# A transformer trunk layer on one core: the weight ring goes from three whole blocks to three half blocks

## The chip, the cores and the metric

The kernel runs on one core of one Trainium2 chip. The metric is the device time of one launch in microseconds (us), lower is better. Before the change the median of three runs is 462.19 us (461.26 to 464.12).

## What is computed

One layer over 256 tokens of 1024 channels, in float32. The input is normalised and multiplied by one wide matrix `w_in`; three mixers work on slices of the product; their outputs are gated, projected and summed; a mixture of 32 experts follows, in four groups of eight, two experts for each token.

```python
xn = rms_norm(x, mix_norm)
(rnn_x, rnn_y, q, kc, vc, ksl, vsl, kwn, vwn, nsa_g, sc_b, sc_c, sc_h, merge_g) = split(xn @ w_in)
y_rnn = gelu(rnn_y) * rg_lru(conv4(rnn_x))
k_cmp, v_cmp = compress_blocks(kc, cmp_w1, ...), compress_blocks(vc, cmp_w1, ...)
y_nsa = g_cmp*Att_cmp + g_sel*Att_sel + g_win*Att_win
y_sc  = sc_b * conv3(sc_c * sc_h)
merged = sum_b sigmoid(gate_b) * (y_b @ P_b)        # P_b: w_rnn_out, w_nsa_out, w_sc_out
x = x + merged @ w_out
x = x + hierarchical_moe(rms_norm(x))               # 32 experts: w_gate, w_up [1024,256], w_down [256,1024]
```

The expert weights are 32 x 3 matrices of 1 MiB each, 96 MiB in all, and all of them are read.

## The kernel before

**Two stretches.** The first (the dense front, up to about 264 us) computes everything up to the router. The second (the experts) runs eight rounds of four experts, here called groups 0 to 7; each needs 8 MiB of gate and up weights and 4 MiB of down weights.

**Blocks and pieces.** The dense weights arrive in *blocks* of 2 MiB (512 columns of 1024 rows; `kvb` is narrower, 280 columns), in the order of the list `LOADS`: q, kva, kvb, rx, cmp, ry, sb, sc, sh, then ga0 gb0 w0, ga2 gb2 w2, ga1 gb1 w1, and wo0, wo1. Every block but cmp is worked on in two halves, the *pieces* (`PIECES`), numbered 0 to 37: q is 0 and 1, kva 2 and 3, kvb 4 and 5, rx 6 and 7, ry 8 and 9, and so on; w1 is 32 and 33, the four last are halves of wo0 and wo1. For float32 precision on TensorE a piece is split in two: ScalarE (ACT) copies it to `wh` (the high part, L750, signals `hi_ready`), VectorE (DVE) subtracts that from the piece to give `wl` (the low part, L1085, signals `lo_ready`). `wh` and `wl` hold two pieces each. TensorE (PE) then does 16 matmuls of 512 columns (or 32 of 256) with the high part and half as many with the low part of each piece (L1630, L1634, L1695). ACT and DVE do their copies at places written out by hand between their other work, so a copy that waits holds up what is written behind it.

**The ring.** `ring` has three slots of one block. All weight loads are issued by SyncE (SP), on its one DMA queue, in program order. Block i goes to slot i % 3 when both halves of block i-3 have been split (`used`: `lo_ready` at least the number of its second piece plus one). The block cmp (`cmp_w1`, rows of 128 floats, so 512 B at a time) is read by PE directly and is a block of the ring as well; it is free when `hidp` is full, the product at L1731. At the beginning SP issues x, q in three DMAs (L508), kva in two (L512), kvb, then waits for slots: rx after piece 1, cmp after piece 3, ry after piece 5, sb after piece 7.

**Expert buffers.** The loads of groups 0 and 1 have places that are partly other tensors' until late: `even[3]`, `even[4]`, `even[5]` are the ring slots 2, 0, 1; `even[0..2]` lie over attention and recurrence scratch; `odd[0..3]` over the split buffers and others. So some loads go early (`odd_half(3, 0)` and `down_half(1, 0, True)` before block sc, at 47 us), some in between, and those that lie in the ring only when the last blocks are through it: `first_group(3)` (2 MiB to `even[3]`), `down_half(0, 0)`, `(0, 2)`, `(0, 1)`, `(0, 3)` (1 MiB each). Gate and up weights of group 2 are issued when PE is through with the same buffer of group 0 (`kpair_done`), and so on for each later group.

**What PE does around it.** In order: q (pieces 0, 1), a small transpose, kva, kvb, transposes of `kdup`, rx, the product with cmp (L1731), transposes of the normalised q and k (L1741, L1747), ry, and so on. The normalised q and k come from DVE, which does them (L1191 to L1197, `qk_normed`) behind the low parts of pieces 6 and 7 and behind `cx` (L1183).

Of the kernel before, what the change touches and what calls it, by code (L numbers as in the profile page):

```python
# [24 lines left out]
P = 128  # L25
S, D = 256, 1024
TT = S // P
KD = D // P
W4 = 512
CT = W4 // P  # L30
# [28 lines left out]
LOADS = (["q", "kva", "kvb", "rx", "cmp", "ry", "sb", "sc", "sh"]  # L59
         + [f"{x}{b}" for b in BR for x in ("ga", "gb", "w")] + ["wo0", "wo1"])  # L60
LI = {n: i for i, n in enumerate(LOADS)}
# [20 lines left out]

SPLIT = [n for n in LOADS if n != "cmp"]

PIECES = [(n, hf) for n in SPLIT[:-2] for hf in range(2)] + [("wo0", 0), ("wo1", 0), ("wo0", 1), ("wo1", 1)]
# [5 lines left out]
MADE = {n: (f"{n}_0", f"{n}_1") if n[0] == "g" else (f"{n}0", f"{n}1") for n in SPLIT if n not in WB}  # L91
# [14 lines left out]
def trunk(nc, x, mix_norm, w_in, rnn_conv_w, rnn_conv_b, rg_wa, rg_ba, rg_wx, rg_bx, rg_lambda,  # L106
# [5 lines left out]
    with ctx:  # L112
# [7 lines left out]
        ring = sb("ring", [P, RING, SLOT])  # L120
# [48 lines left out]
        def part(area, at, shape):  # L169
# [48 lines left out]
                ring[:, 2, :], ring[:, 0, :], ring[:, 1, :]]  # L218
# [45 lines left out]
        slot_full = [sem(f"slot_full{i}") for i in range(RING)]  # L264
# [16 lines left out]
        kva_half, u_low, q_high = sem("kva_half"), sem("u_low"), sem("q_high")  # L281
# [32 lines left out]
        def copies(name):  # L314

            return 2 if name in ("cmp",) else 1

        def slot_count(name):

            i = LI[name]  # L320
            return 16 * sum(copies(LOADS[j]) for j in range(i % RING, i + 1, RING))

# [6 lines left out]

        def loaded(eng, name):  # L330
            eng.wait_ge(slot_full[LI[name] % RING], slot_count(name))

        def slot(name):
            return ring[:, LI[name] % RING, :]

# [7 lines left out]

        def used(eng, name):

            if (name, 1) in PI:
                eng.wait_ge(lo_ready, PI[name, 1] + 1)
            else:
                full(eng, "hidp")
# [16 lines left out]
        def halves(n, parts):  # L366


            name, hf = PIECES[n]
            if name in WB:  # L370
                src = slot(name).rearrange("p (k n) -> p k n", k=CT)[:, :, hf * CB:(hf + 1) * CB]
                return src, parts[:, n % 2, :].rearrange("p (k n) -> p k n", k=CT)
            w = {"kvb": KVB}.get(name, CB)
            src = slot(name)[:, hf * KH * w:(hf + 1) * KH * w].rearrange("p (k n) -> p k n", k=KH)
            return src, parts[:, n % 2, 0:KH * w].rearrange("p (k n) -> p k n", k=KH)
# [16 lines left out]
        def _(sp):  # L392
            def columns(name, c0, n):
                dst = slot(name)[:, 0:KD * n].rearrange("p (k n) -> p k n", k=KD)
                sp.dma_start(dst, win_v[:, :, c0:c0 + n]).then_inc(slot_full[LI[name] % RING], 16)

            def whole(name, w):
                dst = slot(name)[:, :].rearrange("p (k n) -> p k n", k=CT)
                sp.dma_start(dst, w[0].rearrange("(k p) n -> p k n", p=P)).then_inc(slot_full[LI[name] % RING], 16)

# [85 lines left out]
            for i, name in enumerate(LOADS):  # L486

                if name == "sc":
                    odd_half(3, 0)
                    down_half(1, 0, True)  # L490
                if name == "w2":
                    sp.wait_ge(yl_ready, 1)
                    down_half(1, 1, True)
                if name == "gb1":
                    sp.wait_ge(y_sc_ready, 1)
                    first_group(2)
                if name == "w1":
# [4 lines left out]
                if i >= RING:  # L502
                    used(sp, LOADS[i - RING])
                if name == "q":

                    dst = slot(name)[:, :].rearrange("p (k n) -> p k n", k=KD)
                    for k0, k1, done in ((0, 2, q_quarter[0]), (2, 4, q_quarter[1]), (4, 8, slot_full[0])):
# [1694 lines left out]
```

## Time and profile before

| what | value |
|---|---|
| median of three runs | 462.19 us (461.26 to 464.12) |
| span of the profiled execution, first to last instruction | 459.2 us |
| PE busy | 413.9 us, 90% of the span, 2701 matmuls |
| DVE, ACT, POOL busy | 217.9, 173.8, 40.0 us |
| HBM read | 144.83 MB, 318 GB/s over the span |
| SP's queue | 143.50 MB, 81.0% of 16 engines' span |
| mean granted TensorE clock | 0.959 of full speed |

A busy PE is a PE with matmuls in flight. A DMA share of 1.0 means that all 16 DMA engines moved data all the time. What matters is which of the two is full in which stretch, and what the queue holds at a given moment: transfers of one queue land in the order of their issue.

### The profile page before, as it was taken

How to read it: one execution, taken by the hardware profiler on the slowest of the kernel's cores; microseconds unless marked ns; L12 is line 12 of the kernel's file. 1: busy time of each engine (PE TensorE's matmuls, PEld its weight loads, DVE VectorE, ACT ScalarE, POOL GpSimd, SP SyncE). 2: the span in 40 equal slices, each digit the busy share in tenths (PEclk: the TensorE clock that was granted, in tenths of full speed). 3: DMA queues.
4: the chain of work that ended last, by engine and by line, in shares of the span. 5: the costliest groups of instructions: out<-in, count | busy, mean ns of one | idle time of the engine just before them, and what ended most of it. 6: DMA issues, size and time to landing. Idle time of an engine off the chain costs nothing.

```text
span 459.2 us, 6635 instructions
## 1 busy us (share of the span) xinstructions
PE 413.9 (90%) x2701; PEld 292.7 (64%) x2701; DVE 217.9 (47%) x336; ACT 173.8 (38%) x270; POOL 40.0 (9%) x66
## 2 busy tenths in 40 slices
PE   6999999999999999999999999999929659299586
PEld 3889999999878787888888853535512413225122
DVE  5658988487799994564584650211100201002011
ACT  6558429873764565344256331110201101002001
POOL 8420490000000000000003100000000000000000
PEclk9999999999999999999999899999968959889799
DMA  8997893254552578897589989999999999999996
GB/s 291 348 260 257 327 387 105 100 184 184 183 183 93 185 250 298 286 410 266 183 364 359 387 355 425 423 421 420 428 424 421 422 422 425 424 414 414 400 394 220
DMA packets 43613, 146.27 MB, mean 319 GB/s; under 512 B 2908, under 2 KB 6097, under 8 KB 34242
## 3 DMA queue, kind: packets, MB, share of 16 engines
q1 hardware_dynamic: 42272, 143.50, 81.0%
q10 hardware_dynamic: 562, 1.84, 1.1%
q0 software_dynamic: 752, 0.55, 0.5%
q8 instruction: 19, 0.31, 0.3%
q14 instruction: 8, 0.07, 0.0%
HBM read 144.83 MB, written 1.05 MB: 318 GB/s over the span
## 4 chain that ended last, share of the span: by engine, by line
PE 62%; SPq 15%; DMA 14%; DVE 5%; ACT 2%; issue 2%; DVEq 0%
PE psum L1634 17%; DMA ring<-in_exp_w_down 10%; PE psum L1630 10%; PE psum L1877 7%; SPq L413 6%; PE psum L1927 5%; SPq L461 3%; PE psum L2145 3%; PE psum L2048 3%; DMA a_att<-in_exp_w_down 3%; SPq L429 3%; PE psum L1695 2%; SPq L418 2%; PE psum L2017 2%; PE psum L1769 1%
## 5 line engine op out<-in xcount | busy, mean ns | idle before, releaser
L1085 DVE TENSOR_TENSOR wl<-ring,wh 128x2048 fp32r<-128x2048 f32 (+1 forms) x38 | 85.1, 2245 | 36.5 <-ACT wh L750 35.8
L750 ACT CAST wh<-ring 128x2048 fp32r<-128x2048 f32 (+1 forms) x37 | 69.1, 1868 | 52.6 <-PE psum L1634 21.0
L1574 DVE COPY mix<-psum 128x512 f32<-128x512 f32 (+1 forms) x8 | 5.3, 658 | 115.7 <-PE psum L2145 110.0
L1634 PE MATMUL psum<-wh,x_parts 128*128 128x512 f32 (+1 forms) x256 | 58.1, 379 | 0.2 <-ACT a_att L877 0.2
L1634 PEld LDWEIGHTS psum<-wh,x_parts 128*128 128x128 f32 x256 | 46.0, 188 | 9.1 <-issue 0.4
L1035 ACT COPY mix<-psum 128x512 f32<-128x512 f32 x8 | 4.7, 586 | 103.5 <-PE psum L2145 100.4
L2048 PE MATMUL psum<-a_att,mix 128*32 128x512 f32 x96 | 25.6, 693 | 18.0 <-DMA a_rnn<-in_exp_w_up 17.0
L1630 PE MATMUL psum<-x_parts,wh 128*128 128x256 f32 x320 | 40.5, 284 | 0.0
L1630 PEld LDWEIGHTS psum<-x_parts,wh 128*128 128x128 f32 x320 | 39.1, 192 | 0.1
L2048 PE MATMUL psum<-odd,mix 128*32 128x512 f32 x192 | 24.2, 661 | 10.0 <-DMA odd<-in_exp_w_up 8.8
L2145 PE MATMUL psum<-ring,a_moe 128*32 128x512 f32 x152 | 27.6, 658 | 5.1 <-DMA ring<-in_exp_w_down 5.1
L1634 PE MATMUL psum<-wl,x_parts 128*128 128x512 f32 (+1 forms) x128 | 30.1, 377 | 0.0
L2048 PEld LDWEIGHTS psum<-a_att,mix 128*32 128x32 f32 x96 | 7.0, 126 | 34.0 <-issue 34.0
L2017 PE MATMUL psum<-a_moe,tok 128*128 128x128 f32 x224 | 26.3, 275 | 0.3 <-DVE a_moe L1546 0.3
L2097 PE MATMUL psum<-mix,a_moe 128*128 128x512 f32 x56 | 26.3, 607 | 0.0
L1634 PEld LDWEIGHTS psum<-wl,x_parts 128*128 128x128 f32 x128 | 23.2, 188 | 4.4
L2017 PEld LDWEIGHTS psum<-a_moe,tok 128*128 128x128 f32 x224 | 25.6, 192 | 0.5 <-DVE a_moe L1546 0.5
L2048 PE MATMUL psum<-a_rnn,mix 128*32 128x512 f32 x48 | 25.5, 693 | 0.0
L2048 PE MATMUL psum<-ring,mix 128*32 128x512 f32 x48 | 25.5, 693 | 0.0
L2048 PEld LDWEIGHTS psum<-odd,mix 128*32 128x32 f32 x192 | 7.5, 120 | 24.5 <-issue 24.5
L729 POOL TENSOR_TENSOR tok<-a_rnn,a_att 128x512 f32<-128x512 f32 x4 | 5.2, 1300 | 183.3 <-DVE a_rnn L1448 179.9
L1630 PE MATMUL psum<-x_parts,wl 128*128 128x256 f32 x160 | 20.8, 283 | 0.0
(319 smaller groups left out, 629.7 us busy)
## 6 DMA issues: line engine op xcount, KB each, us to landing
ring<-in_w_in SPq DMA_DIRECT2D x11, 2048.0 KB, 7.8
ring<-in_exp_w_down SPq DMA_DIRECT2D x19, 1024.0 KB, 15.8
odd<-in_exp_w_gate SPq DMA_DIRECT2D x12, 1024.0 KB, 14.8
odd<-in_exp_w_up SPq DMA_DIRECT2D x12, 1024.0 KB, 16.8
a_att<-in_exp_w_gate SPq DMA_DIRECT2D x8, 1024.0 KB, 14.9
a_att<-in_exp_w_up SPq DMA_DIRECT2D x8, 1024.0 KB, 16.9
mix<-in_exp_w_down SPq DMA_DIRECT2D x6, 1024.0 KB, 27.6
a_rnn<-in_exp_w_gate SPq DMA_DIRECT2D x4, 1024.0 KB, 21.4
```

What stands on the lines that cost most here:

```text
L413: sp.dma_start(dst[:, m], src).then_inc(is_full, 16)
L429: sp.dma_start(odd_third[:, c, :], src).then_inc(down_third[1], 16)
L750: a.copy(high, src).then_inc(hi_ready, 1)
L1085: signal(v.tensor_tensor(low, src, halves(m, wh)[1].bitcast(fp32), ALU.subtract), lo_ready, m + 1)
L1630: ins = t_.matmul(bank(name)[:, c * S:(c + 1) * S], wv[:, k, ct * P:(ct + 1) * P], xp[hf][:, k, :], start=start, stop=stop, skip_group_che ...
L1634: ins = t_.matmul(bank(name)[:, 0:n], xp[hf][:, k, i * P:(i + 1) * P], wv[:, k, :], start=start, stop=stop)
L1877: ins = t_.matmul(bank(name), yp[:, k, t * P:(t + 1) * P], w[:, k, :], start=first and k == 0, stop=last and k == CT - 1)
L1927: ins = t_.matmul(bank(name), xp[hf][:, k, t * P:(t + 1) * P], wv[:, k, :], start=kk == 0 and xp is xh and not low, stop=kk == KD - 1 and ...
L2017: ins = t_.matmul(xo[:, b, k * P:(k + 1) * P], tok[:, t, (4 * b + k) * P:(4 * b + k + 1) * P], hv[:, t, :], start=t == 0, stop=t == TT - 1)
L2048: ins = t_.matmul(h_ps[e * SLOTS:(e + 1) * SLOTS, :].rearrange("p (m f) -> p m f", m=2), xg[:, k, e * SLOTS:(e + 1) * SLOTS], ws[e][:, k], ...
L2097: return t_.matmul(y_ps[t][hf], hotT[:, t, :], o_sb[:, hf * CB:(hf + 1) * CB], start=False, stop=False, skip_group_check=True)
L2145: ins = t_.matmul(xo[e * SLOTS:(e + 1) * SLOTS, hf, :], hT[:, c, e * SLOTS:(e + 1) * SLOTS], wd[e][:, c, hf * CB:(hf + 1) * CB], start=c == 0,
```

## The change

`ring` keeps its size. Its last 1.5 slots become three places of *half* a block, one for each piece. The first slot holds the compression weights cmp and is given to `even[3]` when `hidp` is full; the half slot behind it is never used by the ring and is the first half of `even[4]`.

- Each piece is its own DMA (1 MiB; w blocks by column halves). Piece m waits for `lo_ready` of piece m-3. In blocks: before, a block was issued when the block three before it was through; now a piece when the piece three before it is through.
- cmp leaves the list of blocks. Its two DMAs are issued right after piece 2 (the first half of kva), without a wait.
- `odd_half(3, 0)` is issued behind piece 3, `down_half(1, 0, True)` behind piece 4, `down_half(0, 0)` behind piece 5. Before, the first two stood before block sc, the third near the end.
- `first_group(3)` stands before piece 12 (the first half of sc), behind the wait for `hidp`. Before, it stood behind the last block.
- The other interleaved loads (`down_half(1, 1, True)`, `first_group(2)`, `first_group(0)` and `(1)`) move from before the blocks w2, gb1, w1 to before the pieces 23, 27, 31.
- ACT waits for the piece's own semaphore before each copy. PE, DVE and GpSimd run the same instructions.

```diff
@@ loads
-LOADS = (["q", "kva", "kvb", "rx", "cmp", "ry", "sb", "sc", "sh"]
+LOADS = (["q", "kva", "kvb", "rx", "ry", "sb", "sc", "sh"]
-        ring = sb("ring", [P, RING, SLOT])
+        ring = sb("ring", [P, 3 * SLOT])
+        HALF = SLOT // 2
+        PIECES_AT = 3 * SLOT - RING * HALF
+        cmp_weights = ring[:, 0:SLOT]
-                ring[:, 2, :], ring[:, 0, :], ring[:, 1, :]]
+                ring[:, 0:SLOT], ring[:, SLOT:2 * SLOT], ring[:, 2 * SLOT:]]
+        def piece_at(m):
+            return ring[:, PIECES_AT + (m % RING) * HALF:][:, 0:HALF]
@@ sync
+            def load_piece(m):
+                if m >= RING:
+                    sp.wait_ge(lo_ready, m - RING + 1)
+                name, hf = PIECES[m]
+                dst = halves(m, wh)[0]
...
+                    sp.dma_start(dst, piece_source(name, hf)).then_inc(piece_full[m % RING], 16)
+            for m in range(len(PIECES)):
+                if m == PI["ry", 0] + 4:
+                    full(sp, "hidp")
+                    first_group(3)
+                if m == PI["ga2", 1]:
                     sp.wait_ge(yl_ready, 1)
                     down_half(1, 1, True)
+                if m == PI["w2", 1]:
                     sp.wait_ge(y_sc_ready, 1)
                     first_group(2)
+                if m == PI["gb1", 1]:
                     full(sp, "o3")
                     first_group(0)
                     first_group(1)
+                load_piece(m)
+                if m == RING - 1:
+                    load_cmp()
+                if m == PI["kva", 1]:
+                    odd_half(3, 0)
+                if m == PI["kvb", 0]:
+                    down_half(1, 0, True)
+                if m == PI["kvb", 1]:
+                    down_half(0, 0)
-            used(sp, "w1")
-            first_group(3)
-            sp.wait_ge(lo_ready, PI["wo0", 0] + 1)
-            down_half(0, 0)
             sp.wait_ge(merged_ready, 4)
             odd_half(3, 1)
             sp.wait_ge(lo_ready, PI["wo1", 0] + 1)
-            down_half(0, 2)
+            down_half(0, 3)
...
-            down_half(0, 3)
+            down_half(0, 2)
@@ scalar
-                    if n == 2:
-                        act.wait_ge(kva_half, 16)
-                    elif n in (1, 3) or PIECES[n][1] == 0:
-                        loaded(act, PIECES[n][0])
+                    act.wait_ge(piece_full[n % RING], piece_count(n))
@@ tensor
-            loaded(pe, "cmp")
+            pe.wait_ge(cmp_full, 32)
```

## Rows read from the trace of the kernel before

**Rows 1.** Busy us (and count) by engine in a stretch; clock, DMA share, GB/s.
```profile
11.00:264.00 253.00, 252.14 (x1569) 219.37 (x1570) 184.72 (x254) 139.58 (x212) 30.24 (x33) 0.99 0.71 255
268.00:448.00 180.00, 143.25 (x1028) 64.95 (x1023) 22.88 (x56) 23.22 (x37) 0.00 (x0) 0.91 1.02 418
```

**Rows 2.** The same by 4 us: the end of the front, and a pause of PE.
```profile
240.00:244.00 4.00, 4.00 (x19) 3.32 (x18) 2.82 (x3) 2.48 (x3) 0.00 (x0) 1.00 0.66 231
...
264.00:268.00 4.00, 4.00 (x38) 1.51 (x40) 2.29 (x11) 2.23 (x7) 0.00 (x0) 1.00 0.71 258
...
332.00:336.00 4.00, 1.76 (x16) 1.57 (x14) 1.02 (x2) 0.73 (x2) 0.00 (x0) 1.00 1.02 432
336.00:340.00 4.00, 0.00 (x0) 0.00 (x0) 0.00 (x0) 0.00 (x0) 0.00 (x0) 0.66 1.01 422
...
344.00:348.00 4.00, 4.00 (x28) 1.17 (x24) 0.00 (x0) 0.00 (x0) 0.00 (x0) 0.56 1.01 409
```

**Rows 3.** Timeline of SP's queue: start us, us, what is issued.
```profile
184.66 0.37 SPq L448 DMA_DIRECT2D a_att<-in_exp_w_gate  x1
...
219.78 0.37 SPq L448 DMA_DIRECT2D ring<-in_exp_w_gate  x1
...
266.55 0.33 SPq L413 DMA_DIRECT2D a_att<-in_exp_w_gate  x1
```

**Rows 4.** Timeline of PE at the beginning: start us, us.
```profile
27.80 3.79 PE L1634 MATMUL psum<-wh,x_parts 128*128 128x512 f32 x16
...
40.23 4.07 PE L1630 MATMUL psum<-x_parts,wh 128*128 128x256 f32 x32
```

**Rows 5.** Timeline of ACT: start us, us (idle before it, and its end).
```profile
22.90 1.92 ACT L750 CAST wh<-ring 128x2048 fp32r<-128x2048 f32 x1
...
35.55 1.91 ACT L750 CAST wh<-ring 128x2048 fp32r<-128x2048 f32 x1 [0.16 <-issue]
39.12 0.19 ACT L809 ACTIVATE a_att<-psum 128x24 f32<-128x24 f32 x1 [1.67 <-PE psum L1634]
...
39.73 0.37 ACT L810 COPY a_att<-psum 128x256 f32<-128x256 f32 x1
...
204.64 1.91 ACT L750 CAST wh<-ring 128x2048 fp32r<-128x2048 f32 x1 [3.48 <-PE psum L1634]
```

**Rows 6.** Timeline of DVE: start us, us.
```profile
12.48 6.85 DVE L1085 TENSOR_TENSOR wl<-ring,wh 128x2048 fp32r<-128x2048 f32 x3 [0.26 <-ACT wh L783]
24.85 2.29 DVE L1085 TENSOR_TENSOR wl<-ring,wh 128x2048 fp32r<-128x2048 f32 x1 [5.51 <-ACT wh L750]
...
40.63 2.29 DVE L1085 TENSOR_TENSOR wl<-ring,wh 128x2048 fp32r<-128x2048 f32 x1
```

**Rows 7.** The chain that ended last, around the transposes of q.
```profile
52.40 1.55 DVE a_att L1197 x4
54.00 1.09 PE psum L1741 x8
```

**Rows 8.** kva's two DMAs (L512); kvb's and rx's (L395, 8 to 20 us).
```profile
L512 SPq DMA_DIRECT2D ring<-in_w_in x2: 536/784/1032, 3.6 to 4.2; - x2
...
DMA to landing us min/median/max: 11.1/12.6/14.1
...
L395 SPq DMA_DIRECT2D ring<-in_w_in x2: 368/1831/3294, 5.3 to 17.0; - x2
DMA to landing us min/median/max: 12.0/14.6/17.2
```

**Rows 9.** cmp's two DMAs (L519), issue and landing.
```profile
L519 SPq DMA_DIRECT2D ring<-in_cmp_w x2: 857/1200/1542, 27.2 to 28.5; - x2
...
DMA to landing us min/median/max: 6.6/8.3/9.9
```

**Rows 10.** The stretch in which cmp passes, and the landing of `down_half(0, 0)` (1 MiB).
```profile
30.00:38.00 8.00, 8.00 (x53) 7.42 (x52) 4.00 (x14) 4.96 (x9) 2.24 (x7) 1.00 1.00 261
...
DMA to landing us min/median/max: 5.4/5.4/5.4
```

More of the change, by code:

```diff
@@ L81 @@
 BK["xT1"], BK["xT2"] = BK["xT2"], BK["xT1"]
-SPLIT = [n for n in LOADS if n != "cmp"]
-PIECES = [(n, hf) for n in SPLIT[:-2] for hf in range(2)] + [("wo0", 0), ("wo1", 0), ("wo0", 1), ("wo1", 1)]
+PIECES = [(n, hf) for n in LOADS[:-2] for hf in range(2)] + [("wo0", 0), ("wo1", 0), ("wo0", 1), ("wo1", 1)]
 PI = {p: i for i, p in enumerate(PIECES)}
@@ L89 @@
 WB = [f"w{b}" for b in BR]
-MADE = {n: (f"{n}_0", f"{n}_1") if n[0] == "g" else (f"{n}0", f"{n}1") for n in SPLIT if n not in WB}
+MADE = {n: (f"{n}_0", f"{n}_1") if n[0] == "g" else (f"{n}0", f"{n}1") for n in LOADS if n not in WB}
 MADE.update(wo0=("wo0", "wo2"), wo1=("wo1", "wo3"))
@@ L261, in trunk @@
         count_ps = h_ps[:, 0:E]
-        slot_full = [sem(f"slot_full{i}") for i in range(RING)]
+        piece_full = [sem(f"piece_full{i}") for i in range(RING)]
+        cmp_full = sem("cmp_full")
         even_full = [sem(f"even_full{i}") for i in range(NDOUBLE)]
@@ L311, in trunk, with piece_count @@
             "xg_act", "xg_dve", "o_act", "o_dve", "y_ready", "y_act", "stored"))
[L314 to L321, printed above, removed]
+        def piece_count(m):
+            return 16 * (m // RING + (m % RING > 0))
+        def piece_at(m):
+            return ring[:, PIECES_AT + (m % RING) * HALF:][:, 0:HALF]
         def place(j, odd_group):
@@ L392, in _, with piece_source, load_cmp @@
         def _(sp):
[L393 to L399, printed above, removed]
+            AT = dict(q=C_Q, kva=C_KC, kvb=C_KWN, rx=C_RX, ry=C_RY, sb=C_SB, sc=C_SC, sh=C_SH)
+            def piece_source(name, hf):
+                if name in WB:
+                    w = (w_rnn_out, w_nsa_out, w_sc_out)[int(name[1])]
+                    return w[0].rearrange("(k p) n -> p k n", p=P)[:, :, hf * CB:(hf + 1) * CB]
+                rows = slice(hf * KH, (hf + 1) * KH)
+                if name[0:2] == "wo":
+                    c0 = int(name[2]) * CB
+                    return w_out[0].rearrange("(k p) n -> p k n", p=P)[:, rows, c0:c0 + CB]
+                c0 = C_MG + int(name[2]) * D + (name[1] == "b") * CB if name[0] == "g" else AT[name]
+                return win_v[:, rows, c0:c0 + {"kvb": KVB}.get(name, CB)]
+            def load_piece(m):
[3 more added lines that the diff above has]
+                dst = halves(m, wh)[0]
+                if m == 0:
+                    for i in range(2):
+                        k = slice(2 * i, 2 * i + 2)
+                        sp.dma_start(dst[:, k], piece_source(name, hf)[:, k]).then_inc(q_quarter[i], 16)
+                else:
+                    sp.dma_start(dst, piece_source(name, hf)).then_inc(piece_full[m % RING], 16)
+            def load_cmp():
+                for kv in range(2):
+                    sp.dma_start(cmp_weights[:, kv * LP * P:(kv + 1) * LP * P].rearrange("p (l n) -> p l n", l=LP),
+                                 cmp_w1[0, kv].rearrange("(l p) n -> p l n", p=P)).then_inc(cmp_full, 16)
             def down_sem(e, odd_group):
```

54 lines of the change are left out of this document (3 added, 51 removed).

## The prediction

> **What bounds the kernel now.** I read the windows by engine first. Between 11 and 264 us PE is busy 252.1 of 253 us, while the DMA engines are 71% busy; from 268 to 448 us it is the other way round, PE 143 of 180 us and the DMA share 1.02 at 418 GB/s [rows 1]. So the kernel is two stretches end to end: a front bound by PE and a tail bound by the transfer of expert weights. A load taken from the front or put into it matters only if PE then waits, or if the tail can begin earlier.
>
> Next, what joins them. The tail's first new transfer, group 2's first gate block, is issued at 266.55 [rows 3], because it needs a buffer that PE has finished reading for group 0. Every later group is released in the same way. The queue is not full to the end before that: its share is 0.66 in 240 to 244 us and 0.71 in 264 to 268 [rows 2]. Loads issued in the front have therefore passed when the tail starts; what is left at 266 us comes from loads issued after about 241 us, which wait for PE to release their buffers and which the change doesn't move. Hence the end is the time at which PE finishes the front, plus a tail that doesn't change.
>
> Last, the start, where PE, ACT and DVE run close together. PE takes piece 3 (second half of kva) at 27.80 and piece 6 (first half of rx) at 40.23 [rows 4]. ACT copies these at 22.90 and 35.55, 1.92 us each, so piece 3 has about 3 us to spare and piece 6 has 2.8 [rows 5].
>
> **What the change removes.** It takes 3 MiB from the queue between 220 and 236 us: `first_group(3)`, issued at 219.78 [rows 3], and `down_half(0, 0)` behind it. At the tail's rate of 418 GB/s [rows 1] a MiB (1.049 MB) takes 2.5 us, so this is 7.5 us of queue. I cost it at zero: between them and the tail the queue runs empty (0.66 at 240 to 244 us, rows 2), and PE is busy throughout. Were the queue full from 220 to 266 us, the gain would be up to 7.5 us.
>
> **What it costs later in the front.** A piece is now issued when the piece three before it has been split. The 1 MiB of `down_half(0, 0)` landed in 5.4 us [rows 10], and a piece occupies PE for about 5.7 us (3.79 for the high part and half as much for the low part, rows 4). The copies run up to two pieces ahead of PE, so of the three pieces of lead one is left, and that just covers a landing. The worst place is piece 31, now behind the four DMAs of `first_group(0)` and `(1)` and piece 30: 5 MiB from 184.66 [rows 3] plus itself are 6 x 2.5 = 15 us, plus the 2.9 us by which 5.4 exceeds 2.5, so 202.6 against a copy at 204.64 [rows 5]. It fits. The 2 MiB of `first_group(3)` before piece 12 add 5 us where the queue is half empty. I take zero for all of this; the bound is 2.8 us at piece 31, should the 6 MiB go at 3.3 us each (184.66 + 19.8 + 2.9 = 207.4), and that stays within the lead of ACT's copy over PE, which is 4.7 us at piece 6 (35.55 against 40.23, rows 4, 5).
>
> **What it costs at the start.** The order of transfers was x, q, kva, kvb, rx, cmp. Now it is x, q, piece 2, cmp, piece 3, expert MiB, piece 4, expert MiB, piece 5, expert MiB, piece 6. All of it is issued before the queue can run empty: piece 3 when piece 0 is split (12.48 + 2.29 = 14.8, rows 6), and piece 6 when piece 3 is. So the queue is in one line, and the landing times add.
> - Piece 2 lands at 3.6 + 11.1 = 14.7, as before; piece 3 landed at 4.2 + 14.1 = 18.3, so 3.5 us a MiB with the small GpSimd loads beside it. kvb landed at 5.3 + 17.2 = 22.5, 4.2 us for both halves, so 2.1 each. rx landed at 17.0 + 12.0 = 29.0, which is 3.25 us a MiB [rows 8].
> - cmp: 8.0 us pass at 261 GB/s for 2.10 MB [rows 10]; by landings, 27.2 + 6.6 = 33.8 and 28.5 + 9.9 = 38.4, thus 4.6 each, 9.2 together [rows 9]. I take 8.6.
> - The pieces of w_in: between 2.5 (the tail's rate) and 3.5; I take 3.0, since fewer of the small loads are left by then. Expert weights: 2.5.
>
> The Trainium skill (DMA: Bandwidth & Descriptors, Specifications) gives 512 B as the smallest transfer that reaches line rate. cmp's rows are just that, and this trace disagrees: 261 GB/s against 418. By the page alone cmp would take 5.0 us, and piece 6 would land 3.6 us earlier.
>
> Piece 3 lands at 14.7 + 8.6 + 3.0 = 26.3, its high part is there at 28.2, and PE, which wants it at 27.80, waits 0.4 us. This is contained in what follows. Piece 6 lands at 26.3 + 2.5 + 2.1 + 2.5 + 2.1 + 2.5 + 3.0 = 41.0; high part 42.9; PE wants it at 40.23, so it stands 2.7 us. Behind this copy ACT has the copies of kvb from PSUM (39.12 to 40.10, 1.0 us, rows 5), and DVE waits for them before piece 6's low part: 43.9 instead of 40.63 [rows 6], 3.3 us late. From there DVE works without a break to the normalised q and k, for which PE waits at 54.00 [rows 7]. So the whole is 3.3 us late there, of which 2.7 were already lost at piece 6. Nothing takes it back: PE has 0.9 us without work in 253.
>
> Bounds: with 8.0 for cmp and 2.5 a MiB, piece 6 lands at 39.4, and the loss is 1.7 us. With 9.2 and 3.5 it lands at 42.6, and the loss is 4.9 us.
>
> **Sum.** Profiled execution: 459.2 + 3.3 = 462.5. That span lies 3.0 us below the median of the runs, and I take the difference as constant: 462.2 + 3.3 = 465.5 us.
>
> **Rivals.**
> - *Hidden (no change).* If cmp passes at the rate of its neighbours (3.0 us a MiB, so 6.0 instead of 8.6), piece 6 lands at 38.4, its high part is there at 40.3, DVE begins at 41.3: 0.7 us, 462.9. For it: the pair was measured beside other small loads. Against it: 261 GB/s over 8 us. The Trainium skill's line-rate figure above would make this the outcome.
> - *Faster.* The 3 MiB taken out let the later loads, and with them the tail, come earlier: 462.2 - 7.5 = 454.7. It decides only if the queue has no gap from 220 us to the tail. The shares 0.66 and 0.71 [rows 2] and the issue at 266.55 right behind PE's release [rows 3] speak against it.
> - *Slower, by the clock.* PE's granted clock stayed at 1.00 in 332 to 336 us with PE busy 1.76 of 4 us, was 0.66 in the 4 idle us that followed, and 0.56 in 344 to 348 us with PE fully busy [rows 2]: PE had stood for about 2.2 us at the full clock when it fell, somewhere in the next 4, to the lower of its two levels (1.2 of 2.4 GHz), and the first 4 us back at work cost about 2. The stand at piece 6 is 2.7 us, 4.3 in the upper bound, so it is in doubt. If the clock falls, 465.5 + 2 = 467.5, up to 470 with the upper bound.
> - *Slower, by a ring too short later.* If a piece in the middle landed in 8 us instead of 5.4, as the blocks of 2 MiB do, each piece would lose up to 2 us of ACT's lead; TensorE has two more in hand. I give it no number beyond the bound above and count it with the clock: 468 or more.
>
> **How the numbers follow.** Forecast (loss of 1.7 to 4.9 us) 0.52; hidden 0.18; slower by clock or short ring 0.24; faster 0.06. A measurement of this kernel tells about 1% (4.6 us) from no change, so the bounds are 457.6 and 466.8. Slower by over 1%: the second pair's 0.22 and the forecast's uppermost part 0.08, so 0.30. Faster 0.06. Within 1%: 0.64. The range goes from below "hidden", 461.8, to 469.0, which takes in the clock's 467.5; it leaves out "faster" (0.06) and some 0.12 at both ends.
>
> **What would show it.** Right: PE standing 2 to 4 us before piece 6 at about 43 us, released by ACT's copy, itself by a DMA; a shorter stand before L1741; the expert loads of group 2 issued at about 270; DMA shares near 0 around 220 to 230 us; the same tail. Wrong: cmp landing before 21 us (hidden); the issue for group 2 at 266 or earlier with a shorter tail (faster); a granted clock below 1 in 40 to 50 us, or PE standing anywhere between 60 and 250 us (slower).

## The result, and the profile after

The changed kernel took 468.24 us, median of 6 runs (467.26 to 470.17), against 462.13 us (461.26 to 464.12) for the kernel before on the same chip: ratio 1.0121, 95% interval 1.0093 to 1.0149. Measured once more later, together with some of the experiments, it took 466.98 us against 462.87: ratio 1.0088 (1.0058 to 1.0118). So the change costs 4 to 6 us, about 1%. (A ratio given here can differ in the third decimal from that of the two medians.)

| | before | after |
|---|---|---|
| median | 462.13 us | 468.24 us |
| span of the profiled execution | 459.2 us | 465.2 us |
| first matmul with expert weights | 264.56 us | 269.18 us |
| from there to the end | 194.6 us | 196.0 us |

I call the time of that first matmul the *end of the front*, and what follows it the *tail*. Of the 6.0 us by which the spans differ, 4.6 are lost in the front and 1.4 in the tail. Where in the front? The changed kernel's timeline of PE around pieces 3 and 6 (start us, us, instruction; in brackets the idle time before it and what ended it):

```profile
25.80 1.98 PE L1612 MATMUL psum<-wl,x_parts 128*128 128x512 f32 x8
30.14 5.53 PE L1612 MATMUL psum<-wh,x_parts 128*128 128x512 f32 x16 [2.36 <-ACT wh L728]
35.50 1.98 PE L1612 MATMUL psum<-wl,x_parts 128*128 128x512 f32 x8
...
43.52 1.04 PE L1695 MATMUL psum<-ident,a_att 128*128 128x128 f32 x8
44.83 4.06 PE L1608 MATMUL psum<-x_parts,wh 128*128 128x256 f32 x32 [0.27 <-ACT a_att L788]
...
58.47 1.09 PE L1719 MATMUL psum<-ident,a_att 128*128 128x128 f32 x8
```

Line 1612 is the old 1634, 1608 the old 1630, 1719 the old 1741. Piece 3 is taken at 30.14 and not at 27.80, after a stand of 2.36 us; its 16 matmuls then last 5.53 us and not 3.79 [rows 4]. The granted clock is still 1.00 while PE stands and falls to its lower level, 0.50, after PE has taken up work again at 30.14:

```profile
29.00:30.00 1.00, 0.00 (x0) 0.00 (x0) 0.00 (x0) 1.00 (x1) 0.48 (x1) 1.00 1.13 409
30.00:31.00 1.00, 0.86 (x3) 0.68 (x4) 0.88 (x1) 0.08 (x1) 1.00 (x3) 0.71 1.09 433
31.00:32.00 1.00, 1.00 (x4) 0.81 (x3) 1.00 (x1) 0.00 (x0) 1.00 (x3) 0.50 0.95 386
```

(us in the window, busy us by engine, clock, share and GB/s, as in [rows 1].) Piece 6 is taken at 44.83, 4.6 us later than the 40.23 of before. The transposes of q begin at 58.47, 4.5 us later than before [rows 7], and nothing more is lost up to 260 us: the last transposes at L1638 (L1660 of before) begin at 260.22 and not at 255.75, 4.47 us later. The timeline of ACT (L728 is the old L750) says what was late:

```profile
28.19 1.90 ACT L728 CAST wh<-ring 128x2048 fp32r<-128x2048 f32 x1 [5.37 <-DMA ring<-in_w_in]
...
42.43 1.90 ACT L728 CAST wh<-ring 128x2048 fp32r<-128x2048 f32 x1 [2.96 <-DMA ring<-in_w_in]
```

In [rows 5] these two copies begin at 22.90 and 35.55 and don't wait for a DMA. Now ACT stands 5.37 and 2.96 us for the pieces themselves. The chain that ended last, in this stretch (start us, us, what), is in one piece from DMA to DMA:

```profile
15.66 12.51 DMA ring<-in_w_in
...
28.19 1.91 ACT wh L728
...
30.12 2.31 DVE wl L1063
...
32.44 9.97 DMA ring<-in_w_in
...
42.43 1.33 ACT wh L728
```

Piece 3 is issued at 15.66, lands 12.5 us later, is split, and only its low part at 32.42 frees the slot into which piece 6 goes. SP's queue shows why the first takes so long (L403 issues cmp, L399 pieces; below it the landing times of cmp's two DMAs):

```profile
4.10 11.50 SPq L403 DMA_DIRECT2D ring<-in_cmp_w  x2
15.66 5.11 SPq L399 DMA_DIRECT2D ring<-in_w_in  x1
20.81 1.19 SPq L479 DMA_DIRECT2D odd<-in_exp_w_gate  x1
```
```profile
L403 SPq DMA_DIRECT2D ring<-in_cmp_w x2: 1075/5528/9982, 4.1 to 5.6; - x2
...
DMA to landing us min/median/max: 16.8/18.0/19.1
```

cmp lands at 4.1 + 16.8 = 20.9 and 5.6 + 19.1 = 24.7, and piece 3 3.5 us behind it. From 14 to 22 us, in which most of cmp passes, the queue moves 270 GB/s with its share at 1.06 (columns as in [rows 1]):

```profile
14.00:22.00 8.00, 8.00 (x36) 6.36 (x35) 5.13 (x3) 3.60 (x3) 1.75 (x4) 1.00 1.06 270
```

The tail begins later for the same reason: the release of group 2's first buffer, 266.55 in [rows 3], is now at 271.17.

```profile
271.17 0.33 SPq L418 DMA_DIRECT2D a_att<-in_exp_w_gate  x1
```

### The profile page after: what moved, and what is told of

Same layout as the page of the kernel before. It is cut to its first block, busy times and chain, and to the rows that moved or that the text cites. A ratio compares the mean times of both kernels' runs of the same rounds, so it can differ in the third digit from the quotient of the medians.

```text
span 465.2 us, 6652 instructions
## 1 busy us (share of the span) xinstructions
PE 416.7 (90%) x2701; PEld 294.0 (63%) x2701; DVE 217.8 (47%) x336; ACT 173.6 (37%) x270; POOL 39.9 (9%) x66
## 3 DMA queue, kind: packets, MB, share of 16 engines
q10 hardware_dynamic: 562, 1.84, 1.1%
## 4 chain that ended last, share of the span: by engine, by line
PE 56%; DMA 25%; SPq 13%; ACT 2%; DVE 2%; issue 1%; DVEq 0%; ACTq 0%
PE psum L1612 14%; PE psum L1608 13%; DMA ring<-in_exp_w_down 9%; DMA ring<-in_w_in 7%; PE psum L1855 7%; DMA a_rnn<-in_exp_w_up 6%; SPq L418 6%; PE psum L1905 5%; PE psum L2026 4%; SPq L466 4%; PE psum L2123 3%; DMA a_att<-in_exp_w_down 3%; SPq L423 2%; PE psum L1747 1%; PE psum L1827 1%
## 5 line engine op out<-in xcount | busy, mean ns | idle before, releaser
L728 ACT CAST wh<-ring 128x2048 fp32r<-128x2048 f32 (+1 forms) x37 | 69.0, 1865 | 63.0 <-DMA ring<-in_w_in 20.2
L1612 PE MATMUL psum<-wh,x_parts 128*128 128x512 f32 (+1 forms) x256 | 59.8, 387 | 2.6 <-ACT wh L728 2.4
L1612 PEld LDWEIGHTS psum<-wh,x_parts 128*128 128x128 f32 x256 | 47.0, 192 | 12.2 <-ACT wh L728 2.8
L2123 PE MATMUL psum<-ring,a_moe 128*32 128x512 f32 x152 | 28.2, 674 | 6.6 <-DMA ring<-in_exp_w_down 6.6
L1995 PE MATMUL psum<-a_moe,tok 128*128 128x128 f32 x224 | 26.3, 275 | 0.3 <-DVE a_moe L1524 0.3
L2075 PE MATMUL psum<-mix,a_moe 128*128 128x512 f32 x56 | 26.3, 607 | 0.0
```

What stands on the lines that cost most here:

```text
L728: a.copy(high, src).then_inc(hi_ready, 1)
L1612: ins = t_.matmul(bank(name)[:, 0:n], xp[hf][:, k, i * P:(i + 1) * P], wv[:, k, :], start=start, stop=stop)
L1995: ins = t_.matmul(xo[:, b, k * P:(k + 1) * P], tok[:, t, (4 * b + k) * P:(4 * b + k + 1) * P], hv[:, t, :], start=t == 0, stop=t == TT - 1)
L2075: return t_.matmul(y_ps[t][hf], hotT[:, t, :], o_sb[:, hf * CB:(hf + 1) * CB], start=False, stop=False, skip_group_check=True)
L2123: ins = t_.matmul(xo[e * SLOTS:(e + 1) * SLOTS, hf, :], hT[:, c, e * SLOTS:(e + 1) * SLOTS], wd[e][:, c, hf * CB:(hf + 1) * CB], start=c == 0,
```

## The experiments

Theory: the start pays for everything. cmp, 2 MiB in short rows, and the three expert MiB stand ahead of pieces 3 to 6 in one queue. Rivals: the ring of three halves costs by itself; the clock, which falls after PE has stood, makes the greater part of the loss; the loads taken out of 220 to 236 us give something back.

Each edit is shown against the changed kernel; `...` in a diff stands for lines left out. The ratio is to the kernel before, measured beside it. The profiled executions, in one table (the fifth column is the start of the last transposes at L1660 of before; a star marks an execution whose granted clock from 257 to 268 us was 0.84, it was 1.00 in the others):

| kernel | ratio to before (95%) | first 16 matmuls of q, us | piece 3 / 6 taken | last transposes | end of front | tail |
|---|---|---|---|---|---|---|
| before | 1 | 3.94 | 27.80 / 40.23 | 255.75* | 264.56 | 194.6 |
| before, again | 0.9994 (0.9972 to 1.0016) | 5.63 | 29.30 / 41.73 | 257.25 | 265.56 | 195.1 |
| changed | 1.0121 (1.0093 to 1.0149) | 3.92 | 30.14 / 44.83 | 260.22* | 269.18 | 196.0 |
| changed, again | 1.0088 (1.0058 to 1.0118) | 5.76 | 30.20 / 44.94 | 261.77* | 270.74 | 195.8 |
| cmp later | 1.0000 (0.9979 to 1.0022) | 5.62 | 29.79 / 42.22 | 257.75 | 266.06 | 195.5 |
| experts before piece 12 | 1.0072 (1.0046 to 1.0099) | 5.77 | 29.50 / 41.93 | 259.63 | 267.94 | 195.8 |
| experts behind piece 10 | 1.0020 (0.9996 to 1.0045) | 5.55 | 29.04 / 41.47 | 257.29* | 266.26 | 194.9 |
| both later | 1.0018 (0.9995 to 1.0040) | 3.94 | 28.23 / 40.66 | 256.19 | 264.50 | 196.4 |
| ring alone | 1.0077 (1.0054 to 1.0101) | 5.23 | 29.26 / 41.69 | 257.20* | 266.17 | 197.6 |
| PE kept busy | 1.0075 (1.0052 to 1.0098) | 3.92 | 30.19 / 44.53 | 259.98 | 268.29 | 194.9 |
| cmp in long rows | 1.0038 (1.0018 to 1.0057) | 3.92 | 28.23 / 42.71 | 258.15 | 266.47 | 194.7 |
| cmp later, PE warmed | 1.0011 (0.9985 to 1.0037) | 3.94 | 29.10 / 41.53 | 257.12 | 265.44 | 194.8 |

The third column must be read first. The first 16 matmuls of a launch took either 3.9 us or 5.2 to 5.8, in the same kernel from one execution to another. Before this was seen, a front that ended 1 to 1.5 us later could be taken for a cost of the edit. So a front is compared with that execution of before that had a like first pass.

There is a second difference between executions, at the other end of the front. From the last transposes to the end of the front it takes 8.31 or 8.32 us in the seven executions without a star and 8.81 to 8.97 in the five with one. The first and the second profile of before, in one stretch of it (columns as in [rows 1]); the clock is 0.73 in the first and 1.00 in the second:

```profile
260.00:264.00 4.00, 4.00 (x26) 3.88 (x26) 1.67 (x9) 0.22 (x1) 0.00 (x0) 0.73 1.01 428
```
```profile
260.00:264.00 4.00, 3.13 (x25) 2.83 (x25) 2.89 (x16) 0.29 (x1) 0.00 (x0) 1.00 1.02 429
```

Both kernels have it, the one before and the changed one, and what decides it is not known. So what an edit does to the front is read at the last transposes, not at its end. There the change loses 4.47 and 4.52 us in its two profiles, "experts before piece 12" 2.38, "cmp in long rows" 2.40, "experts behind piece 10" 0.04, and "ring alone" nothing.

**The kernel before, again.**

> The kernel before once more, unchanged, to see how much one profiled execution of it differs from another. If the front and tail of an execution are set by the kernel: the first head matmul after the key compression near 264.6 us and a tail of about 194.6 us from there to the end of the span. If the tail differs by a microsecond between executions of one kernel, the 1.2 to 1.4 us by which the changed kernel's two profiled tails are longer than the first one's show nothing; if the tail is again 194.6 us or less, they are the kernel's. Ratio 1.00.

(The "first head matmul after the key compression" of this text is the first matmul with expert weights.) Measured: ratio 0.9994 over 10 runs. With its slow first pass the last transposes began 1.5 us later and the front ended 1.0 us later, and the tail was 195.1, half a microsecond longer than the first. The expectation's two cases for the tail, a microsecond or nothing, leave this value between them.

**cmp later.** The 2 MiB of cmp go behind piece 7:

```diff
-                if m == RING - 1:
-                    load_cmp()
...
+                if m == PI["rx", 1]:
+                    load_cmp()
```

> The changed kernel, with the two DMAs of cmp issued behind piece 7 instead of behind piece 2; the three expert MiB stay between the pieces, first_group(3) stays early. Theory 'start queue' (what stands ahead of pieces 3 and 6 makes PE wait, cmp's 9 us most of all): piece 3 lands near 18 us and piece 6 near 33, PE waits for neither, the first experts' matmuls begin near 264.6 as in the kernel before (269.2 in the changed one), time 462 to 463. Rival 'short ring' (three half places cost time everywhere): still near 466 or more, with waits of PE after 60 us. Rival 'tail' (1.4 of the 6 us arise after 265 us whatever the start does): 463.5 to 464. Rival 'early loads pay' (3 MiB fewer in the crowded stretch bring the tail forward): 455 to 460.

Ratio 1.0000 (0.9979 to 1.0022) over 12 runs: no loss is left that can be seen, with the short ring and the three early expert MiB in place. Pieces 3 and 6 are copied without a wait for a DMA (columns as above):

```profile
24.89 1.92 ACT L728 CAST wh<-ring 128x2048 fp32r<-128x2048 f32 x1
...
37.53 1.92 ACT L728 CAST wh<-ring 128x2048 fp32r<-128x2048 f32 x1 [0.16 <-issue]
...
49.37 1.91 ACT L728 CAST wh<-ring 128x2048 fp32r<-128x2048 f32 x1 [2.99 <-DMA ring<-in_w_in]
```

The last line is piece 8, for which ACT stands 3 us behind cmp; PE, two pieces behind ACT, does not notice. The front ends 0.5 us later than that of before with the like first pass, and PE had begun its first pass 0.46 us later (11.47 against 11.01), so nothing is lost in between.

**Experts before piece 12.** The three expert MiB leave the start and stand before piece 12, with the two of `first_group(3)`:

```diff
                 if m == PI["ry", 0] + 4:
+                    odd_half(3, 0)
+                    down_half(1, 0, True)
                     full(sp, "hidp")
+                    down_half(0, 0)
                     first_group(3)
...
-                if m == PI["kva", 1]:
-                    odd_half(3, 0)
-                if m == PI["kvb", 0]:
-                    down_half(1, 0, True)
-                if m == PI["kvb", 1]:
-                    down_half(0, 0)
```

> The changed kernel, with cmp early as there, but the three expert MiB that stood between the pieces 3 to 6 moved to before piece 12, beside first_group(3). Theory 'start queue': piece 3 still lands near 28, because only cmp and piece 3 itself are ahead of it; PE stands 2.4 us and the clock falls as before; piece 6, issued when piece 3 is split at 32.4, lands near 38 and is no longer awaited; PE loses 4.1 instead of 4.6 us, time 467.5 to 468. If instead the expert loads are what delays PE: 463 or less.

Ratio 1.0072 (1.0046 to 1.0099), a median of 466.09 us, between the expectation's two forecasts, and for another reason. The start is good (piece 6 at 41.93, 0.2 us behind before's 41.73), but a new wait has come. ACT's copy of piece 12 stands for its DMA, behind 5 MiB in one go, and PE stands 1.84 us for what ACT does next:

```profile
83.25 1.91 ACT L725 CAST wh<-ring 128x2048 fp32r<-128x2048 f32 x1 [2.39 <-DMA ring<-in_w_in]
```
```profile
90.74 2.18 PE L1605 MATMUL psum<-x_parts,wh 128*128 128x256 f32 x16 [1.84 <-ACT mix L875]
```

The shift of PE against before goes from 0.2 to 2.4 us at this place and stays. So the short ring isn't free either: ahead of piece 12 it forgives the 2 MiB of `first_group(3)`, as the change has it, but not 5 MiB.

**Experts behind piece 10.** The same three MiB one piece earlier, apart from those of `first_group(3)`, which come some 12 us later; cmp early as in the change:

```diff
-                if m == PI["kva", 1]:
+                if m == PI["sb", 0]:
                     odd_half(3, 0)
-                if m == PI["kvb", 0]:
                     down_half(1, 0, True)
-                if m == PI["kvb", 1]:
                     down_half(0, 0)
```

> As e2_experts_later, but the three expert MiB are issued behind piece 10 (46 us), where the queue has a gap, instead of together with first_group(3) before piece 12. cmp stays early. In e2 piece 12 landed behind 5 MiB and cost PE 2 us at 88 us; here it must not. Left is what cmp alone does to piece 3. Theory 'piece 3 and piece 6 are two delays of which the later counts': piece 3 lands at 26.5 to 28, PE stands 1 to 2.4 us there (none where the first matmuls were slow), piece 6 is in time; loss against the kernel before 1 to 4 us, time 463.5 to 466. If the expert MiB were all of it: 462.

Ratio 1.0020 (0.9996 to 1.0045). With cmp early and the experts out of the way, ACT still waits 2.45 us for piece 3, but piece 6 is there at 37.09, in time:

```profile
26.70 1.91 ACT L726 CAST wh<-ring 128x2048 fp32r<-128x2048 f32 x1 [2.45 <-DMA ring<-in_w_in]
...
37.09 1.91 ACT L726 CAST wh<-ring 128x2048 fp32r<-128x2048 f32 x1 [0.18 <-DMA ring<-in_w_in]
```

So neither load costs much without the other; together they cost 4.5 us of the front. With one of the two, piece 6 is there at 37.5 us or earlier, ACT's turn in these executions, and PE takes it 4 to 5 us after ACT begins its copy; with both it lands at 42.4.

For cmp alone this holds with a reserve. This execution had the slow first pass, which put PE's turn for piece 3 at 29.04. With a first pass of 3.92 it would have been at 27.4, and the high part is there at 26.70 + 1.91 = 28.6: an estimate of 1.2 us of stand, which the interval of the ratio allows (up to 1.0045, 2.1 us) and no profile here shows.

**Both later.** cmp behind piece 7 and the three MiB behind piece 10.

```diff
-                if m == RING - 1:
+                if m == PI["rx", 1]:
                     load_cmp()
-                if m == PI["kva", 1]:
+                if m == PI["sb", 0]:
                     odd_half(3, 0)
-                if m == PI["kvb", 0]:
                     down_half(1, 0, True)
-                if m == PI["kvb", 1]:
                     down_half(0, 0)
```

> Both the compression weights (behind piece 7) and the three half blocks of expert weights (behind piece 10) moved out of the start. Theory that the start's loss is only the queueing of these 5 MiB ahead of pieces 3 and 6: no piece of the first ten waits, ratio 0.995 to 1.001, like the runs with one of the two moved. Rival, that the three-half ring costs by itself: at least 1.003. Rival, that a burst of 5 MiB before pieces 8 to 11 makes one of them late as the burst before piece 12 did: a wait of ScalarE for piece 11 of 2 us and more, a loss of about 2 us (ratio 1.004), which is likely hidden only if the ring is three pieces ahead there.

Ratio 1.0018 (0.9995 to 1.0040); the interval doesn't shut out the rival's 1.003, so the profile has to decide. ACT waits 3.03 us for piece 8 behind cmp, which the expectation had excluded, and PE for no piece; ACT doesn't wait for piece 11. The last transposes come 0.44 us after those of before, as much as PE's first pass began later (11.49 against 11.07). The end of the front:

```profile
264.50 3.64 PE L2009 MATMUL psum<-a_att,mix 128*32 128x512 f32 x32
```

So the ring of three halves by itself costs nothing in the front that these profiles show, when no more than two or three MiB stand ahead of a piece. The tail of this execution is 196.4 us, the second longest; see below.

**Ring alone.** cmp behind piece 7, and all expert loads as late as the free space allows, near where they stood before:

```diff
                 if m == PI["ry", 0] + 4:
+                    odd_half(3, 0)
+                    down_half(1, 0, True)
                     full(sp, "hidp")
-                    first_group(3)
...
-                if m == RING - 1:
+                if m == PI["rx", 1]:
                     load_cmp()
...
+            first_group(3)
+            sp.wait_ge(lo_ready, PI["wo0", 0] + 1)
+            down_half(0, 0)
             sp.wait_ge(merged_ready, 4)
```

> The ring of three half places alone: cmp behind piece 7, odd_half(3, 0) and down_half(1, 0, True) before piece 12, first_group(3) and down_half(0, 0) at the end, as in the kernel before. Theory 'start queue': like the kernel before, 462 to 463, and like e1_cmp_later within 1 us, because the early loads bring nothing and cost nothing once the start is clear. Rival 'short ring': 464 or more. Rival 'early loads pay': slower than e1_cmp_later by 2 to 7 us. Rival 'tail': 463.5 to 464.

Ratio 1.0077 (1.0054 to 1.0101), a median of 465.98 us. 'Start queue' missed; the time is that of 'short ring' (464 or more) and of 'early loads pay' (3.0 us above "cmp later"), and the trace shows a mixture of the two. The front is good (last transposes at 257.20, before's at 257.25; first pass 5.23). But SP's program order puts `first_group(3)` behind the load of the last piece, which in a ring of three halves waits for a late slot: it is issued at 232.84, not at 219.78 [rows 3]. The queue is then full from there across the release of the tail:

```profile
240.00:252.00 12.00, 12.00 (x63) 10.08 (x62) 5.65 (x6) 7.69 (x13) 2.60 (x2) 1.00 1.03 415
...
264.00:268.00 4.00, 3.84 (x37) 2.50 (x40) 1.24 (x7) 2.45 (x7) 0.00 (x0) 1.00 1.01 420
268.00:272.00 4.00, 4.00 (x44) 1.21 (x40) 3.61 (x18) 0.00 (x0) 0.00 (x0) 1.00 1.01 412
```

In [rows 2] the share at 264 to 268 is 0.71. Here it is 1.01, so the tail's loads stand behind a backlog, and the tail is 197.6 us, 2.5 to 3.0 longer than in the kernel before. This is what the early loads buy: in the change they pay no gain, they avoid this loss, which the short ring creates.

**PE kept busy.** Ten matmuls of 512 columns on data that is there, before the wait for piece 3, into a bank that nobody reads:

```diff
+                        if m == PI["kva", 1] and low == 0:
+                            for _ in range(10):
+                                t_.matmul(psum[:, 6, :], xh[0][:, 0, 0:P], xh[0][:, 0:2, :], start=True, stop=True)
                         pe.wait_ge((hi_ready, lo_ready)[low], m + 1)
```

> The changed kernel, with ten more matmuls of 512 columns on PE before the wait for piece 3, into a PSUM bank that nothing reads then; the output is unchanged. They fill PE's pause at 27.8 us with work (10 x 0.23 = 2.3 us). Theory 'the clock falls because PE stands': the granted clock stays at 1.00 in 30 to 34 us and the 16 matmuls of piece 3 take 3.8 us instead of 5.5. What this is worth: if piece 6 is late by itself (issued when piece 3 is split at 32.4, landed at 42.4), PE only waits there instead, and the time stays at 468.2; if the clock's 1.7 us are a loss of their own, 466.5.

Piece 3's pass takes its usual 3.79 us, and the 1.7 us are gone, yet piece 6 is taken at 44.53 and not at 44.83, because it is itself late:

```profile
30.19 3.79 PE L1615 MATMUL psum<-wh,x_parts 128*128 128x512 f32 x16
...
44.53 4.07 PE L1611 MATMUL psum<-x_parts,wh 128*128 128x256 f32 x32 [1.67 <-ACT a_att L788]
```

What the clock takes at piece 3 PE would have stood at piece 6 anyway, so far as the profile goes: the last transposes begin at 259.98 and not at 260.22. (Piece 3 itself had landed 1.7 us earlier in this execution, at 26.5, and piece 6 came at 42.1 all the same.) The time says less clearly the same. The median, 465.75 us, lies at the 466.5 of the other theory and not at 468.2, and the ratio, 1.0075 (1.0052 to 1.0098), below the change's 1.0121 and 1.0088 without being clearly apart from the second. Between the two profiles, only 0.24 us of the difference arise before 260 us; 0.65 are the clock at 257 to 268 us and 1.1 the tail, and both differ between executions of one kernel too.

**cmp in long rows.** The same 2 MiB in rows of 8 KB, one per partition, in place of 512 B. The weights then lie in another order, so the compression product isn't the reference's; all else is the same.

```diff
-                                 cmp_w1[0, kv].rearrange("(l p) n -> p l n", p=P)).then_inc(cmp_full, 16)
+                                 cmp_w1[0, kv].rearrange("(p l) n -> p l n", p=P)).then_inc(cmp_full, 16)
```

> The changed kernel with cmp_w1 read as 8 KB rows, one for each partition, instead of sixteen rows of 512 B: the same bytes to the same place, in another arrangement, so that the compression product is computed with permuted weights. Theory 'cmp is slow because of its 512-byte rows': it passes in 5 us instead of 9, piece 3 lands near 23 and is not awaited, piece 6 lands at 37 to 38.5, time 462 to 463.5. If the amount of bytes ahead of piece 6 counts and not cmp's slowness: 465 or more.

```profile
L403 SPq DMA_DIRECT2D ring<-in_cmp_w x2: 964/966/968, 4.7 to 5.7; - x2
...
DMA to landing us min/median/max: 15.0/16.0/17.1
```
```profile
25.39 1.91 ACT L728 CAST wh<-ring 128x2048 fp32r<-128x2048 f32 x1 [1.96 <-DMA ring<-in_w_in]
...
40.31 1.90 ACT L728 CAST wh<-ring 128x2048 fp32r<-128x2048 f32 x1 [4.49 <-DMA ring<-in_w_in]
```

Issuing the pair costs SP 2 us, not 11.5. cmp's second half lands at 5.7 + 17.1 = 22.8. Piece 2 had landed at 15.6 in this execution, so the pair takes 7.2 us; in the five profiled executions with cmp in the same place and short rows it takes 8.9 to 9.1. Piece 6 is copied at 40.31, against 42.13 to 42.54 in the three with the same loads. So the short rows are worth 2 us of the loss, and the ratio falls to 1.0038 (1.0018 to 1.0057), a median of 464.22 us, between the expectation's two forecasts; cmp's bytes and the expert MiB are the rest: PE still takes piece 6 2.5 us later than before (42.71 against 40.23). At the 418 GB/s of [rows 1] the pair would pass in 5.0 us. Of the 3.9 us by which the short rows exceed that, the row length is 1.7 to 1.9; the other 2.2 stay with long rows.

The Trainium skill (DMA: Bandwidth & Descriptors, Specifications) lets transfers of 512 B go at line rate. The two kernels differ in nothing but the row length, and by 1.7 to 1.9 us for the pair, so the runs disagree with the page.

**The changed kernel, again.**

> The changed kernel once more, to separate what belongs to it from what differs between executions. Theory 'start queue': PE stands before piece 3 or piece 6, the first experts' matmuls begin 4 to 5 us after the kernel before, the tail after that is 194.6 to 196 us as in both; time 466 to 468.5. If the tail itself is longer: 196 us or more again.

Ratio 1.0088. The copies of pieces 3 and 6 wait as in the first profile, to 0.1 us (28.24 and 42.54). The clock falls at another place, in the pass of piece 6, which PE had taken at 44.94 after a stand of 1.93 us:

```profile
44.94 5.56 PE L1608 MATMUL psum<-x_parts,wh 128*128 128x256 f32 x32 [1.93 <-ACT a_att L788]
```
```profile
45.00:46.00 1.00, 1.00 (x8) 1.00 (x9) 0.77 (x1) 0.89 (x2) 0.00 (x0) 0.84 0.53 199
46.00:47.00 1.00, 1.00 (x6) 1.00 (x6) 1.00 (x1) 1.00 (x1) 0.00 (x0) 0.50 0.16 61
```

A granted clock of 0.50 is the lower of the two levels. Here nothing covers the loss: against the second profile of before, PE is 3.2 us late when it takes piece 6 and 4.7 us when it is done with its high part. So the two profiles reach the same 4.5 us in two ways. Piece 6 lands at the same time in both, and the slow first pass of this one has already used up 1.5 us of the lateness (before's own turn was 41.73 and not 40.23); the clock puts 1.5 back.

**cmp later, PE warmed.** As "cmp later", with five and three small matmuls before the first block, to see whether the slow first pass can be avoided.

```diff
+            for _ in range(5):
+                t_.matmul(psum[:, 6, 0:P], ones[:, :], ones[:, :], start=True, stop=True)
...
+                if i == 3:
+                    for _ in range(3):
+                        t_.matmul(psum[:, 6, 0:P], ones[:, :], ones[:, :], start=True, stop=True)
```

> e1_cmp_later with eight small matmuls of ones into an unread PSUM bank in PE's idle time before the first block. In the profiles of e1, e2 and e3 the first 16 matmuls took 5.2 to 5.8 us, in the others 3.9, at a recorded clock of 1.00 in both. Theory 'PE is not yet at full speed when the first block starts, by chance': with the filler they take 3.9 always, time 461 to 462, 1 us under e1 and under the kernel before. Otherwise as e1, 462 to 463.

The first pass took 3.94 us but began at 12.37 and not at 11.47, and the ratio is 1.0011 (0.9985 to 1.0037), a median of 463.83 us and not 461 to 462: no gain that can be seen. Whether the matmuls or chance made the pass quick, one profile doesn't say.

No version beats the kernel before. The best, "cmp later", can't be told from it.

## Why the prediction was right or wrong

The forecast was 465.5 us, from a loss of 3.3; measured were 468.24 and 466.98, losses of 6.1 and 4.1. The direction held, and so did the mechanism: the loads put ahead in one queue make piece 6 late, and nothing makes up for it. One term, the landing of piece 6, was sized too small. And the forecast by itself, a loss of 1.7 to 4.9 us, doesn't reach the first measurement, 6.1; that lies inside the range only through the room left for the clock. Of the 6.0 us between the two profiles 4.6 are the front, within the bound, and 1.4 a tail that was said to be the same.

- **The tail follows the front; the 3 MiB taken out at 220 us are worth nothing.** Held. "Both later" has all of these loads early, a front as before and no gain. The queue's gap was there, somewhat later than I had said: the share is 0.70 at 220 to 224 us and 0.19 at 228 to 232, since the last pieces of a shorter ring are loaded later.

```profile
220.00:224.00 4.00, 4.00 (x19) 3.32 (x18) 2.03 (x1) 2.89 (x3) 0.00 (x0) 1.00 0.70 258
...
228.00:232.00 4.00, 4.00 (x23) 3.40 (x22) 1.10 (x3) 0.70 (x2) 0.00 (x0) 1.00 0.19 74
```

- **The short ring costs nothing later.** Held for the change: PE is 4.5 us late at the transposes of q and 4.47 us at the last ones. Piece 31 was indeed close: ACT copied it 5.2 us later than before and not 4.5, after 4.22 us of standing for its DMA, and piece 23 5.0 us later; PE noticed neither. But a larger burst ahead of another piece is worse: 5 MiB before piece 12 cost 2 us in "experts before piece 12". I had worked out one place and taken it for the worst.
- **Piece 3: landing 26.3, a wait of 0.4.** In the three experiments with the same order up to it, it landed at 26.4 to 26.9, and in the two without the filler PE did not wait. That was luck: both had the slow first pass, which put PE's turn for piece 3 at 29.0 and 29.5 and not at 27.8. In both profiles of the change it landed at 28.2 to 28.3, because piece 2 came at 15.8 and not at 14.7 (1.1), cmp took 8.9 and not 8.6 (0.3), and piece 3 took 3.5 behind it and not 3.0 (0.5). cmp took 8.9 to 9.1 in all five with short rows. What makes piece 2 come at 14.8 in one execution and 15.8 in another is open. Because of this the long stand of the first profile was at piece 3, 2.36 us, and before piece 6 PE stood only 0.27; the sign I had named, 2 to 4 us before piece 6, came in neither profile (1.93 in the second).
- **Piece 6: landing 41.0.** This is the term that was mis-sized. It landed at 42.4 and 42.5 in the change and at 42.1 in "PE kept busy". In the change the sum is 15.8 + 8.9 + 3.5 + 14.2 = 42.4, with the filler 14.8 + 8.9 + 2.7 + 15.7 = 42.1, in the forecast 14.7 + 8.6 + 3.0 + 14.7 = 41.0. The parts move against each other, since the queue is one line; the whole is 1.1 to 1.5 us longer than I had it. In the change the excess arises by piece 3 (1.9 us, as above), and what stands behind piece 3 was even 0.5 shorter than I had it; with the filler it is the other way round, and that part is 1.0 longer.
- **DVE begins piece 6's low part at 43.9, 3.3 late, and that carries to the end.** It began at 45.13, 4.5 late. The transposes at L1719 were 4.5 late and the last ones before the router 4.47. The 1.2 us come from the landing, and the lateness was carried through as I had said, though not by DVE alone: in the kernel before the chain that ended last reaches these transposes through DVE [rows 7], in the change through PE's own matmuls from piece 6 on, with DVE done at 58.41, 0.04 us before PE. The upper bound (cmp at 9.2, 3.5 a MiB, piece 6 at 42.6, a loss of 4.9) came nearer than the forecast.
- **Slower, by the clock.** I had made it a rival, from a reading that was too coarse: taken by the microsecond, the kernel before has its clock at 1.00 up to 337 us and at 0.63 in 337 to 338, so PE, which had stopped at 333.8, had stood some 3.5 us when it fell, not 2.2. By that row the stands here would have looked harmless; the rival came about in both profiled executions of the change. In both the clock was at 1.00 while PE stood and fell some 0.3 and 0.7 us after it had taken up work again. At piece 3, where PE stood 2.36 us, it cost 1.7 us of pass, but with the clock kept by the filler PE took piece 6 only 0.3 earlier. At piece 6, after 1.93 us, it cost 1.5 with nothing to cover it. The forecast's price of 2 was about right, but it is a matter of the execution: after stands of 1.67 and 1.80 us at the same piece, in "PE kept busy" and "cmp in long rows", the pass took 4.07 and 4.06 us.
- **Hidden, if cmp goes at its neighbours' rate.** I had said 0.7 us for that case. With long rows PE took piece 6 2.5 us late. So even that rival's own sum was low: the pair took 7.2 us there, not 6.0 (1.2 us), and piece 2 before it came at 15.6 and not at 14.7 (0.9 us).
- **The same tail.** Open. It was 1.4 us longer in the first pair of profiles and 0.6 in the second. The other kernels with early expert loads lie from 194.7 to 196.4, and each has one profile only, so these can't tell a cost from chance. The queue's share falls at the release in all of them but "ring alone". In five of them (the two of the change, "cmp later", "both later", "experts before piece 12") the rate dips for two or more microseconds once the release's first transfers run, as in "both later" here (1 us each; the mean of the tail of before is 418, [rows 1]); what makes it I don't know.

```profile
270.00:271.00 1.00, 1.00 (x16) 0.26 (x8) 0.45 (x3) 0.00 (x0) 0.00 (x0) 1.00 0.86 279
...
272.00:273.00 1.00, 0.77 (x7) 0.78 (x7) 0.17 (x1) 0.99 (x2) 0.00 (x0) 1.00 0.83 303
```

## What to carry to other kernels

A load that is moved ahead is paid by what stands behind it in the same queue at that moment; ask of the first pieces, where nothing has a lead yet, before asking how much room a load finds on average. Two moves that each fit into the lead may not fit together: sum them at the same consumer. In a ring with less depth, look at every place where a burst stands ahead of a piece, and ask whether the program order of the issuing engine pushes other loads back behind the last slot.

## What the runs showed of the hardware

- Issuing can block. In the change cmp's second DMA held SP for 9.98 us, and piece 3's for 5.11; the five behind them took 1.19, 0.49, 0.55, 0.47 and 3.35. With 8 KB rows cmp's two took 0.97 each, but there too two later ones, of long rows, took 1.90 and 4.65. In the kernel before, where the queue's share was 0.49 and 0.26 in the two microseconds in which they were issued (27 to 29), they took 0.86 and 1.54 [rows 9]. What stands behind such an issue in SP's program, a wait for a slot too, is reached later.
- Row length alone: 2 MiB in rows of 512 B took 8.9 to 9.1 us, in rows of 8 KB 7.2, with the same transfers around them; while most of the short rows passed, from 14 to 22 us, the queue moved 270 GB/s at a full share, with long rows 341.
- The clock can fall after a short stand, and after the stand is over: PE stood 2.36 and 1.93 us in the two profiles of the change at a granted clock of 1.00, and the clock went to 0.50 once it worked again. After 1.67 and 1.80 us in two other kernels it didn't fall.
- The first 16 matmuls of a launch took 3.9 us or 5.2 to 5.8, with the granted clock recorded as 1.00 in both. In the second profile of before:

```profile
11.01 5.63 PE L1695 MATMUL psum<-wh,x_parts 128*128 128x512 f32 x16 [0.19 <-ACT wh L783]
```
```profile
12.00:14.00 2.00, 2.00 (x6) 1.60 (x5) 1.75 (x2) 2.00 (x2) 2.00 (x4) 1.00 1.06 387
```

Six matmuls fall into 2 us there, at a recorded clock of 1.00, where the 16 of a usual pass take 3.8. It moves PE's turn for piece 6 by 1.5 us between the two profiles of before, as much as the effects looked for, and must be read off each profile before two of them are compared.
